# RWKV scan: fewer waits ahead of the exponentials and the matmuls, the key-rate product on GpSimd, and the opening's sum of squares on VectorE

## The reference

```
h = rmsnorm(x, w) * (1.0 + scale) + shift
...
kk = heads(k * k_k);  kk = kk / max(sqrt(sum(kk * kk)), 1e-12)
k_dir = k * (1.0 + (icl - 1.0) * k_a)
...
def step(S, inp):
    r_t, w_t, k_t, v_t, kk_t, a_t = inp
    sa = einsum('bdhvk,bdhk->bdhv', S, -kk_t)
    S = S * w_t[..., None, :] + sa[..., None] * (kk_t * a_t)[..., None, :] + v_t[..., None] * k_t[..., None, :]
    return S, einsum('bdhvk,bdhk->bdhv', S, r_t)
```

## Time and profile before

| | |
|---|---|
| median of three runs | 4566.91 us (4566.62 to 4568.85) |
| the profiled execution | 4574.58 us, its span 4572.7 us, mean granted clock 0.966 |
| TensorE busy | 4107.4 us (90%) |
| TensorE weight loads busy | 3528.4 us (77%) |
| VectorE busy | 2634.2 us (58%) |
| ScalarE busy | 1943.5 us (43%) |
| GpSimd busy | 92.4 us (2%) |

### The profile page before, as it was taken

One profiled execution on the slowest core, in us unless ns is written; L12 is line 12 of the kernel. 1 busy time (PEld: TensorE's weight loads), 2 busy tenths in 40 slices (PEclk: granted clock), 3 DMA queues, 4 the chain that ended last, 5 costly groups with the idle time before them and its releaser, 6 DMA issues. The chain is left out here.

```text
span 4572.7 us, 133471 instructions
## 1 busy us (share of the span) xinstructions
PE 4107.4 (90%) x58784; PEld 3528.4 (77%) x58784; DVE 2634.2 (58%) x4521; ACT 1943.5 (43%) x3640; POOL 92.4 (2%) x82
## 2 busy tenths in 40 slices
PE   6999978998887899899998999889999788888978
PEld 2888867877775799666668899877988677777758
DVE  5433557777775643355556433467425477777755
ACT  5333325555554531455554000145333255555542
POOL 0000000000110000000000000000000000001100
PEclk9999989999998899899999999999999889999989
DMA  7444765334434131100000221112346843334341
GB/s 300 147 129 130 223 197 144 93 94 101 98 75 160 69 73 43 53 1 1 1 16 23 97 97 67 53 62 69 118 133 187 250 129 103 99 88 100 86 152 61
DMA packets 541152, 471.09 MB, mean 103 GB/s; under 512 B 30113, under 2 KB 501409, under 8 KB 532897
## 3 DMA queue, kind: packets, MB, share of 16 engines
q1 hardware_dynamic: 389152, 387.03, 26.6%
q10 hardware_dynamic: 131840, 66.07, 5.0%
q0 software_dynamic: 19584, 9.44, 2.2%
HBM read 328.50 MB, written 128.71 MB: 100 GB/s over the span
## 5 line engine op out<-in xcount | busy, mean ns | idle before, releaser
L654 PE MATMUL ps<-big_r,stage_r 128*128 128x384 f32 x2976 | 640.0, 350 | 15.7 <-DVE big_r L916 14.3
L654 PEld LDWEIGHTS ps<-big_r,stage_r 128*128 128x128 f32 x2976 | 522.3, 189 | 71.0 <-issue 25.7
L2559 PE MATMUL ps<-big_r,w_out 128*128 128x384 f32 x2304 | 417.5, 341 | 35.9 <-DVE w_out L2675 35.4
L2559 PEld LDWEIGHTS ps<-big_r,w_out 128*128 128x128 f32 x2304 | 406.6, 191 | 45.0 <-DVE w_out L2675 38.6
L654 PE MATMUL ps<-big_r,w_slab_r 128*128 128x384 f32 x1488 | 341.3, 337 | 0.0
L371 PE MATMUL ps<-big_r,stage_r 128*128 128x384 f32 x1536 | 311.0, 337 | 13.7 <-DVE big_r L358 13.6
L1698 DVE COPY_PREDICATED arena<-arena,ps 128x128 f32<-128x128 uint32 x720 | 195.1, 328 | 207.1 <-PE ps L1313 204.6
L2281 DVE TENSOR_REDUCE extra<-ps 128x1 f32<-128x1152 f32 (+1 forms) x144 | 177.7, 1234 | 204.7 <-PE ps L2186 204.7
L371 PEld LDWEIGHTS ps<-big_r,stage_r 128*128 128x128 f32 x1536 | 269.8, 188 | 29.1 <-issue 26.7
L1338 PE MATMUL ps<-ident,arena 128*128 128x128 f32 x1152 | 186.7, 285 | 103.9 <-ACT arena L1520 103.2
L654 PEld LDWEIGHTS ps<-big_r,w_slab_r 128*128 128x128 f32 x1488 | 268.0, 189 | 0.0
(11 more groups left out here) (257 smaller groups left out, 8046.0 us busy)
## 6 DMA issues: line engine op xcount, KB each, us to landing
w_slab<-in_w SPq DMA_DIRECT2D x138, 512.0 KB, 3.5
arena<-scan_in SPq DMA_DIRECT2D x144, 320.0 KB, 3.7
arena<-scan_in SPq DMA_DIRECT2D x288, 128.0 KB, 3.8
scan_in<-x_resid ACTq DMA_DIRECT2D x48, 576.0 KB, 4.6
arena<-scan_in SPq DMA_DIRECT2D x48, 576.0 KB, 6.7
arena<-scan_in SPq DMA_DIRECT2D x144, 192.0 KB, 3.9
arena<-in_w_ada SPq DMA_DIRECT2D x24, 1024.0 KB, 6.0
x_resid<-in_w_ada SPq DMA_DIRECT2D x24, 1024.0 KB, 4.9
```

Source lines behind the costliest of these rows:

```text
L654: mm = pe.matmul(g.ps[:, 3 * s + c, 0:CW], w[:, k * P:(k + 1) * P], x[:, k, chunk(c)], start=k == i == 0, stop=k == NB - 1 and i == 2)
L2559: mm = pe.matmul(g.ps[:, bank(i, b), 0:wide[i]], w[:, b, k * P:(k + 1) * P], r, start=k == j == 0, stop=k == NB - 1 and j == 2)
```

## The change

In the scan, waits are taken out of ScalarE's and TensorE's lists. Piece 0 of the exponentials keeps the waits for cum_ok and r_ok, piece 1 those for d0_ok and a_ok, and pieces 2 to 4 have none. TensorE loses waits in gram, turned_seeds, level_u, level_t and chain_rhs, 14 in the trip of a pair. rate leaves VectorE's list and becomes a tensor_tensor on GpSimd, one pair further ahead, without its factor of -1; decayed_b takes the factor in, as a scalar_tensor_tensor in place of a tensor_tensor. In the opening, VectorE adds up the squares and TensorE sums over channels once, with three products; the matrix of ones is set by VectorE and no longer loaded.

```diff
 phase_open:
-            sp.dma_start(g.ones[:, :], io["ones"]).then_inc(ones_in, 16)
...
                 if b >= 2:
-                    act.wait_ge(sq_used, b - 1)
+                    act.wait_ge(added_ok, max(b - 2, 1))
                 nc.scalar.activation(sq[b % 2], g.x[:, b, :], ACT.Square).then_inc(sq_ok, 1)
...
-            pe.wait_ge(ones_in, 16)
-            norm_matmuls(pe, g, sq, sq_ok, sq_used, 0)
+            pe.wait_ge(set_ok, 5)
+            pe.wait_ge(added_ok, NB - 1)
+            for c in range(CH):
+                pe.matmul(g.ps[:, c, 0:CW], g.ones[:, :], total[:, c * CW:(c + 1) * CW], start=True, stop=True).then_inc(sum_mm, 1)
...
-            dve.wait_ge(sq_used, NB)
+            for b in range(1, NB):
+                dve.wait_ge(sq_ok, b + 1)
+                if b > 1:
+                    dve.wait_ge(added_ok, b - 1)
+                nc.vector.tensor_tensor(total, sq[0] if b == 1 else total, sq[b % 2], op=ALU.add).then_inc(added_ok, 1)
+            dve.wait_ge(sum_mm, CH)
...
 phase_scan, TensorE:
             def gram(q, t):
                 if t == 0:
-                    pe.wait_ge(b_ok, q + 1)
-                    pe.wait_ge(r_ok, q + 1)
-                    pe.wait_ge(k_ok, q + 1)
                     pe.wait_ge(a_ok, q + 1)
...
                 else:
-                    pe.wait_ge(y1_ok, 2 * q + 1)
                     pe.wait_ge(g_ok, 4 * q + 2)
...
             def turned_seeds(q):
-                pe.wait_ge(g_ok, 4 * q + 4)
...
             def level_u(q, k):
-                else:
-                    pe.wait_ge(xa_ok, 4 * q + k - 1)
+                if k == 5:
+                    pe.wait_ge(xa_ok, 4 * q + 4)
...
             def level_t(q, k):
-                pe.wait_ge(xa_ok, 4 * q + k)
-                if q or k > 1:
-                    pe.wait_ge(xt_ok, 5 * q + k - 1)
+                if k < 4:
+                    pe.wait_ge(xa_ok, 4 * q + k)
+                if q and k == 1:
+                    pe.wait_ge(xt_ok, 5 * q)
...
             def chain_rhs(c, step):
                 if c or step:
                     pe.wait_ge(y_ok, 2 * c + step)
-                    pe.wait_ge(sav_ok, 4 * c + 2 * step)
...
 phase_scan, ScalarE:
             def exps(q, i):
-                act.wait_ge(cum_ok, q + 1)
-                if i in (1, 4):
+                if i == 0:
+                    act.wait_ge(cum_ok, q + 1)
+                    if q:
+                        act.wait_ge(r_ok, q)
+                if i == 1:
                     act.wait_ge(d0_ok, q + 1)
-                if q and i < 4:
-                    act.wait_ge(r_ok, q)
-                    act.wait_ge(a_ok, q)
-                    act.wait_ge(k_ok, q)
+                    if q:
+                        act.wait_ge(a_ok, q)
...
 phase_scan, VectorE:
-            def rate(q):
-                if q:
-                    dve.wait_ge(raw_in[q % 2], 96 * loads(q, 2))
-                    dve.wait_ge(b_ok, q)
-                V.scalar_tensor_tensor(bb, raw[q % 2][:, 2048:2560], -1.0, raw[q % 2][:, 512:1024], op0=ALU.mult, op1=ALU.mult).then_inc(bb_ok, 1)
...
-                V.tensor_tensor(strided(bk[q % 2], HD, (256, 4), (1, P)), strided(bb, 0, (P, 4), (1, P)),
-                                strided(ab, P, (256, 4), (1, P)), op=ALU.mult).then_inc(b_ok, 1)
+                V.scalar_tensor_tensor(strided(bk[q % 2], HD, (256, 4), (1, P)), strided(bb, 0, (P, 4), (1, P)), -1.0,
+                                       strided(ab, P, (256, 4), (1, P)), op0=ALU.mult, op1=ALU.mult).then_inc(b_ok, 1)
...
 phase_scan, GpSimd:
+            def rate(q):
+                if q:
+                    pool.wait_ge(raw_in[q % 2], 96 * loads(q, 2))
+                    pool.wait_ge(b_ok, q)
+                nc.gpsimd.tensor_tensor(bb, raw[q % 2][:, 2048:2560], raw[q % 2][:, 512:1024], op=ALU.mult).then_inc(bb_ok, 1)
+
+            for q in range(3):
+                rate(q)
             for c in range(PAIRS):
+                if c + 3 < PAIRS:
+                    rate(c + 3)
                 if plain_stores(c) == 2:
                     continue
```

More of the change, by code:

```diff
@@ L217, in phase_open @@
     ms, root, rstd = g.big[0][:, 0, :], g.big[0][:, 1, :], g.extra[:, 0:T]
+    total = g.big[0][:, 2, :]
     rest = g.arena[:, 2 * NB * T:4 * NB * T]
@@ L228, in phase_open @@
         sem = Sems(nc, ctx)
-        cond_in, ident_in, ones_in, chan_in, next_in, set_ok, sig_ok, silu_ok = sem(
-            "cond_in", "ident_in", "ones_in", "chan_in", "next_in", "set_ok", "sig_ok", "silu_ok")
-        sq_ok, sq_used, ms_ok, root_ok, rstd_ok, tmp_ok, h_ok, h_vector_ok = sem(
-            "sq_ok", "sq_used", "ms_ok", "root_ok", "rstd_ok", "tmp_ok", "h_ok", "h_vector_ok")
+        cond_in, ident_in, chan_in, next_in, set_ok, sig_ok, silu_ok = sem(
+            "cond_in", "ident_in", "chan_in", "next_in", "set_ok", "sig_ok", "silu_ok")
+        sq_ok, added_ok, sum_mm, ms_ok, root_ok, rstd_ok, tmp_ok, h_ok, h_vector_ok = sem(
+            "sq_ok", "added_ok", "sum_mm", "ms_ok", "root_ok", "rstd_ok", "tmp_ok", "h_ok", "h_vector_ok")
         rows_mm, rows_sb, cols_mm, cols_sb, vec_ok = sem("rows_mm", "rows_sb", "cols_mm", "cols_sb", "vec_ok")
@@ L268, in _ @@
             nc.scalar.activation(rstd, root, ACT.Exp, scale=-0.5).then_inc(rstd_ok, 1)
-            act.wait_ge(set_ok, 4)
+            act.wait_ge(set_ok, 5)
             act.wait_ge(rows_mm, 1)
@@ L298, in _ @@
             nc.vector.memset(rows, 0.0).then_inc(set_ok, 1)
-            dve.wait_ge(set_ok, 4)
+            nc.vector.memset(g.ones[:, :], 1.0).then_inc(set_ok, 1)
+            dve.wait_ge(set_ok, 5)
             dve.wait_ge(sig_ok, 1)
             nc.vector.tensor_tensor(g.silu[:, :], cond, sig, op=ALU.mult).then_inc(silu_ok, 1)
-            dve.wait_ge(sq_used, NB)
+            for b in range(1, NB):
[4 more added lines that the diff above has]
+            dve.wait_ge(sum_mm, CH)
             nc.vector.tensor_scalar(as3(ms), slot_view(g.ps[:, 0:3, :]), 1.0 / D, RMS_EPS, ALU.mult, ALU.add).then_inc(ms_ok, 1)
@@ L324, in token_ranges @@
     return ((0, 0, CTX), (1, CTX, T))
-def norm_matmuls(pe, g, sq, sq_ok, used, banks):
-    for b in range(NB):
-        pe.wait_ge(sq_ok, b + 1)
-        for c in range(CH):
-            mm = pe.matmul(g.ps[:, banks + c, 0:CW], g.ones[:, :], sq[b % 2][:, c * CW:(c + 1) * CW],
-                           start=b == 0, stop=b == NB - 1)
-        mm.then_inc(used, 1)
 def take_high(nc, dst, src):
@@ L1763, in _ @@
                     decayed_a(q + 1)
-                if nxt2:
-                    rate(q + 2)
                 if chain:
@@ L2812, in constants @@
     out["ident"] = np.eye(P, dtype=np.float32)
-    out["ones"] = np.ones((P, P), np.float32)
     out["head_ones"] = (row // HD == col // HD).astype(np.float32)
```

## The result

The changed kernel takes 4499.67 us (median of 4 runs, 4498.09 to 4503.28) beside 4567.88 us of the kernel before (4566.62 to 4570.57): a ratio of 0.9851, with an interval of 0.9834 to 0.9868. That is 68 us faster. The forecast was 85 us; the time lies 18 us above its 4482 and inside its range. The profiled execution took 4498.09 us with a span of 4496.2, so in the two profiled executions 4572.7 - 4496.2 = 76.5 us are gone.

A forecast was written before the change was run, and what follows sets the result against it. The prediction took TensorE, nearly full in the scans, to bound the kernel. Its terms, 86.9 - 6 - 3 + 6.9 = 84.8, say 85 us, took the median from 4566.9 to 4482, range 4460 to 4525.

The forecast's parts named there:

- The waits of the exponentials: In the scans, piece 0 without a_ok and k_ok lets copy_x come before TensorE needs it: 86.9 us gained.
- The pauses: TensorE's pauses no semaphore explains, hidden while it waits for copy_x, may show: 6 us given back, bounds 0 and 14.
- The limit of 0.2 us a pair: Sign in the scans: the prediction is wrong if TensorE's unexplained pauses grow by more than 0.2 us a pair.
- the rival of growing pauses: In the scans, TensorE's instruction stream is the limit; half of the 86.9 us comes back as pauses: 4519, chance 0.09.
- The 14 waits of TensorE: In each pair, removed waits are satisfied by one that stays and cost nothing: 0 us; far bound 29 us more gain.
- rate on GpSimd: Product moved off VectorE gains 0; its 1.2 us on GpSimd hold the running sum: 3 us lost, 0 to 19.
- the first rival: At a pair's head GpSimd's product holds VectorE, so level_w ends late: 4531, chance 0.08; or 4565, chance 0.03.
- the slower one built on it: At a pair's head, a GpSimd product of 2.5 us holds VectorE and the kernel gets slower: 4610, chance 0.04.
- The opening: Ahead of the scans, the last h work starts at 40.1 to 41.0, not 47.52: 6.9 us less, 6.5 to 7.4.

The follow-up runs named there:

- the runs with small loads: Changed kernel and kernel before, each with the scan's six loads a pair cut to 8 columns from pair 6 on: 4446.24 us (0.9720) and 4540.91 us (0.9917).

## Why the prediction was right, and where its size was off

*The waits of the exponentials* (86.9 us forecast): 84.6 us by the line of copy_x. The chain was the one described, down to copy_x ready 0.2 us before TensorE wants it (0.26 forecast).

*The pauses* (6 us, bounds 0 and 14): this is the term that was mis-sized. The pauses grew by 0.31 and 0.53 us a pair, 0.42 x 68 = 29 us, and where the exponentials' waits went alone 39 us were given back. The limit of 0.2 us a pair, beyond which the prediction called itself wrong, was passed: on this point it is wrong, although the time lies in its range. The mechanism was named (a stream that catches up while TensorE stands) and priced at 1.3 us times the share 1.3 / 19.7 of a pair, 0.09 us. The wrong base was the pair: as I read the records, a pause is a block that comes late, and blocks come every 4.0 us, so a wait of 1.3 us can cover up to 1.3 / 4.0 of the lateness and not 1.3 / 19.7 of it. The share was not measured by itself, and that it is this fraction is argued; the runs with small loads put what the waits covered at a net 22 us. The evidence used against the rival of growing pauses, one pair without any, was weak: pauses do not come in every pair. The 0.5 us of unexplained idleness in the earlier trace rows should have been followed up over many pairs. That rival gave 4519, from a half of the 86.9 us; by the time the truth is about half way between it and the forecast, and of its 43 us given back 39 were seen with the exponentials' waits alone.

*The 14 waits of TensorE* (0, far bound 29): 13 us alone, 14 put back. The step failed in its ground. The earlier trace rows showed a satisfied wait without a gap where it stands, which is true; its price shows elsewhere, most of it in the pauses. The two errors have opposite signs: 39 us were given back where 6 were forecast, 33 us too many, and 13 us were gained where 0 were forecast. (The 29 us by which the pauses grew in the changed kernel have this gain in them already.) That the time came out 18 us off and not some 30 is luck.

*rate on GpSimd* (0 for VectorE's 0.60 us, 3 us for the hindrance, bounds 0 and 19): 8 us slower alone, nothing measurable in the changed kernel. The product was sized right for the case in which nothing meets it, 1.28 us; it took 1.48 on average and 2.24 at most, above the 1.7 that was forecast as its longest. The new decayed_b costs nothing: 0.65 us on average, as before. The place was right too. VectorE and GpSimd in one pair of the late part of the scan follow. L1640 is decayed_b; L1704, L1685, L1698 and L1693 are the lines that were L1717, L1698 (level_w), L1711 and L1706; L1797 is the product.

```profile
1165.89 0.65 DVE L1640 SCALAR_TENSOR_TENSOR arena<-arena 128x512 f32<-128x512 f32 x1
1166.46 0.28 DVE L1704 TENSOR_TENSOR arena<-arena 128x128 f32<-128x128 f32 x1
1166.75 0.74 DVE L1685 COPY_PREDICATED arena<-arena,ps 128x128 f32<-128x128 uint32 x2
1167.29 0.46 DVE L1698 TENSOR_TENSOR arena<-ps,arena 128x256 f32<-128x256 f32 x1
1167.66 1.86 DVE L1618 TENSOR_TENSOR_SCAN arena<-arena 128x512 f32<-128x512 f32 x1
1169.44 0.69 DVE L1693 COPY arena<-ps 128x512 f32<-128x512 f32 x1
```

```profile
1164.69 2.42 POOL L1810 DMA_DIRECT2D scan_y<-arena  x2 [14.47 <-ACT arena L1560]
1166.69 1.73 POOL L1797 TENSOR_TENSOR arena<-arena 128x512 f32<-128x512 f32 x1
```

The product runs from 1166.69 to 1168.42. L1685 and L1698, with one input in PSUM, keep their lengths of 0.74 and 0.46 (0.73 for level_w in the earlier trace rows, 0.45 for the other in the same pair of before) and their starts; only the running sum, with two tiles in SBUF, is stretched from 1.21 to 1.86. The L1693 behind it has lost its 0.58 us of idleness, which took most of it. Over the whole first scan the COPY_PREDICATEDs of level_w took 328 ns on average before and 329 after, and the TENSOR_TENSORs of 128 by 128 (L1717, now L1704) 283 and 283. So the first rival (level_w held) and the slower one built on it did not come about.

*The opening* (6.9 us): 6.47 by the timeline. The square root came 0.6 us later than forecast (L314 at 28.28, after the end of the forecast's 25.5 to 27.7), which costs nothing since the pieces end it, as foreseen. The difference is the last vectors: h at 41.05, not 40.1 to 41.0.

What stays open is the price of one satisfied wait as an instruction: 32 to 34 ns by taking six from the kernel before or putting them back into the changed one, 39 by adding 27, and 74 by taking away five more, with an interval of some 10 us on each difference. It may not be a price for one wait at all, since the five that went last gained 20 us in one scan and nothing in the other; whether it matters where in the list the borders of the blocks then fall was not tested. How much of it is the sequencer's own 51 ns was not separated.

## What to carry over

A wait that is taken away also hid something. Before pricing its removal, read the "issue" idleness over many pairs and compare the loop from one instruction packet to the next around a pause (here 3.9 us for 256 instructions) with the time TensorE needs for as many (here 3.86). In a list of small products near that limit, count instructions: a satisfied wait opens no gap where it stands, yet taking such waits away was worth more than all the work moved between engines. And move loads or shrink them before cutting further, for through late blocks they cost 60 us here.

## What the runs showed of the hardware

TensorE's clock fell after some of the long pauses. Windows of 1 us of the changed kernel around the pause from 1103.44 to 1105.30:

```profile
1105.00:1106.00 1.00, 0.70 (x26) 0.63 (x28) 0.31 (x2) 0.04 (x1) 0.00 (x0) 1.00 0.07 22
1106.00:1107.00 1.00, 1.00 (x14) 1.00 (x16) 0.77 (x2) 0.69 (x2) 0.00 (x0) 0.68 0.08 18
1107.00:1108.00 1.00, 1.00 (x30) 0.78 (x30) 0.52 (x1) 0.00 (x0) 0.00 (x0) 0.50 0.00 0
```

The granted clock is 1.00, 2.4 GHz, in the window in which TensorE takes up its work, and falls to 0.50, 1.2 GHz, afterwards, for some 3.4 us in all. The 16 products of L1279 take 1.63 us in it where they take 1.16 at 1100.06, and the 32 of L1319 1.13 where they take 0.69. Where this happens, a pause is paid for twice, but it does not happen each time. The changed kernel has seven pauses of over 1.4 us in 60 pairs, and three of them are followed by such a stretch within 1.5 us of their end; three more stretches come without a pause of that length. With the exponentials' waits alone it is six of 13. The kernel before has one such pause, and with the waits for copy_x 45 gaps of over 1.4 us between weight loads, yet only four stretches. What decides it, these runs do not show.

GpSimd's product and VectorE's operations with two inputs in SBUF hinder each other: the running sum took 1.21 us on average before, 1.59 in the changed kernel and at most 2.97; the product 1.28 alone, about 1.73 when it meets the running sum and 2.24 at most. That is the rule of the Trainium skill's "SBUF — State Buffer", section "Who interferes with whom", and the rows agree with it in whom it names, also in that operations with an input in PSUM were left alone. They do not show a plain turn-taking in which the one that comes first keeps its length: the product at 1166.69 came first and took 0.45 us longer than alone, and the running sum behind it 0.65.
